# Filter taps of the long convolution: eight fp32 products become twenty-four single-pass products over 64 rows

## The reference, cut to what matters

```
hdn = sin(fr * (z @ w1 + b1)); hdn = sin(fr * (hdn @ w2 + b2)); hdn = sin(fr * (hdn @ w3 + b3))
h = (hdn @ wout).reshape(length, 2, D_HYENA)         # hdn 512x64, wout 64x1024: the taps
h = h * exp(-t * deltas)[:, None, :]
kern = concatenate([h[:, 0], zeros((1, D_HYENA)), h[:0:-1, 1]], axis=0)
```

## Time and profile before

| what | value |
|---|---|
| median of 3 runs | 1593.58 us (1593.38, 1593.58, 1594.43) |
| profiled execution, span from its first to its last instruction | 1591.6 us (what lies around it is not shown; the median of the runs is 2.0 us more) |
| PE busy | 1582.3 us, 99% |
| DVE, ACT, POOL busy | 62%, 48%, 38% |
| mean granted TensorE clock | 0.999 |
| the stage of the change (step (2, 0) to the sum at (3, 1)) | about 893 to 934 us of the span |

### The profile page before, as it was taken

How to read it: one execution, slowest core, us unless ns; L and a number is a source line. 1 busy time by engine, 2 the same in 40 slices (tenths; PEclk the granted TensorE clock), 3 DMA queues, 4 the chain that set the end, 5 groups by cost and what they waited for, 6 DMA issues and landing times.

```text
span 1591.6 us, 21844 instructions
## 1 busy us (share of the span) xinstructions
PE 1582.3 (99%) x8856; PEld 1360.9 (86%) x8856; DVE 994.1 (62%) x1477; ACT 761.6 (48%) x1143; POOL 603.8 (38%) x301
## 2 busy tenths in 40 slices
PE   9999999999999999999999999999999999999998
PEld 7888898889888888888888777889888789999997
DVE  7888867676765365455553767782356785555554
ACT  7533443343432334555556465424435645555554
POOL 1003112221245334455556333453223225555552
PEclk9999999999999999999999999999999999999999
DMA  6554434343466423233333332132112233232321
GB/s 245 172 172 147 142 117 140 113 132 126 128 214 213 149 70 117 95 106 106 104 96 137 126 120 66 53 107 83 40 54 67 80 106 107 93 106 93 106 93 54
DMA packets 54413, 182.95 MB, mean 115 GB/s; under 512 B 6556, under 2 KB 7196, under 8 KB 53928
## 3 DMA queue, kind: packets, MB, share of 16 engines
q1 hardware_dynamic: 54024, 181.02, 34.6%
q10 hardware_dynamic: 288, 0.52, 0.1%
HBM read 174.42 MB, written 3.96 MB: 112 GB/s over the span
## 4 chain that ended last, share of the span: by engine, by line
PE 92%; DVE 5%; ACT 1%; issue 1%; DMA 0%; SPq 0%; POOL 0%; DVEq 0%; ACTq 0%
PE banks L468 90%; PE banks L471 2%; DVE ACC L1300 1%; DVE wl L1264 1%; DMA maskf<-cst_dram 0%; DVE TM L1858 0%; DVE X L1233 0%; DVE HL L1233 0%; ACT T L2205 0%; DVE XW L2105 0%; ACT wh L2208 0%; ACT HH L2205 0%; DVE banks L1233 0%; DVE TM L1868 0%; ACT FHI L2208 0%
## 5 line engine op out<-in xcount | busy, mean ns | idle before, releaser
L2858 POOL TENSOR_TENSOR wl<-raw,wh 128x1024 fp32r<-128x1024 f32 x139 | 346.8, 2498 | 388.1 <-ACT wh L2208 388.0
L468 PE MATMUL banks<-HH,wh 128*128 128x512 f32 (+2 forms) x944 | 362.2, 386 | 1.3 <-ACT HH L2205 1.0
L468 PE MATMUL banks<-HL,wh 128*128 128x512 f32 (+2 forms) x944 | 353.1, 380 | 0.1
L2208 ACT ACTIVATE wh<-raw 128x1024 fp32r<-128x1024 f32 x246 | 257.3, 1051 | 188.6 <-PE banks L468 184.6
L468 PE MATMUL banks<-HH,wl 128*128 128x512 f32 (+1 forms) x936 | 251.4, 380 | 0.5 <-DVE wl L1264 0.5
L468 PEld LDWEIGHTS banks<-HH,wh 128*128 128x128 f32 (+1 forms) x944 | 177.2, 188 | 38.5 <-issue 2.6
L468 PEld LDWEIGHTS banks<-HL,wh 128*128 128x128 f32 (+1 forms) x944 | 176.6, 188 | 35.5 <-DVE HL L1233 1.7
L468 PEld LDWEIGHTS banks<-HH,wl 128*128 128x128 f32 x936 | 172.1, 188 | 35.8 <-issue 1.5
L468 PE MATMUL banks<-wh,HH 128*128 128x256 f32 x448 | 127.8, 285 | 0.0
L468 PE MATMUL banks<-wl,HH 128*128 128x256 f32 x448 | 126.7, 283 | 0.0
L468 PE MATMUL banks<-wh,HL 128*128 128x256 f32 x448 | 126.7, 283 | 0.0
(11 more groups left out here) (432 smaller groups left out, 3300.1 us busy)
## 6 DMA issues: line engine op xcount, KB each, us to landing
raw<-wst_dram SPq DMA_DIRECT2D x294, 512.0 KB, 3.4
X<-xT_dram SPq DMA_DIRECT2D x8, 512.0 KB, 6.1
CB<-sums_dram SPq DMA_DIRECT2D x12, 256.0 KB, 3.1
D<-dec_dram SPq DMA_DIRECT2D x12, 256.0 KB, 2.9
x_dram<-X SPq DMA_DIRECT2D x3, 512.0 KB, 6.4
QS<-QX SPq DMA_DIRECT2D x24, 64.0 KB, 2.6
KSw<-KX SPq DMA_DIRECT2D x24, 64.0 KB, 2.0
X<-x_dram SPq DMA_DIRECT2D x3, 512.0 KB, 4.6
```

The lines of the kernel that those rows point to most:

```text
L468: return pe.eng.matmul(dst, w, x, start=start, stop=stop, skip_group_check=True)
L2208: return eng.activation(dst, src, ACT.Copy)
L2858: tt(wl[:, q, :], raw[:, i % NRAW, :], wh[:, q, :].bitcast(F32), ALU.subtract).then_inc(*by_pool("low", u))
```

## The change

FO is loaded folded: rows 0 to 63 hold the weights of the forward direction and rows 64 to 127 those of the backward one, 128x512 in place of 128x1024. The third layer's weights and the small vectors are doubled, so that the 64 features stand in FH twice, in rows 0 to 63 and again in rows 64 to 127. After the third sine ACT makes high halves of FH and FO (FHH, FOH). At step (2, 0), ahead of the first taps, DVE makes the low halves (FOL, FHL), in place of FO and FH. PE then makes each block of taps with six fp32r products over 64 rows: for each of high x high, low x high and high x low, one for each direction, side by side.

```
--- before.py
+++ after.py
@@ -358,7 +358,9 @@
 
     UR, US = at("UR", [128, 4, T], C0), at("US", [128, 4, T], C0 + 8)
     FW = at("FW", [128, 3, 128], C0 + 18)
-    FO, FH, EN = at("FO", [128, 1024], 156), at("FH", [128, T], 160), at("EN", [128, T], 162)
+    FO, FH, EN = at("FO", [128, T], 156), at("FH", [128, T], 160), at("EN", [128, T], 162)
+    FOH, FOL = at("FOH", [128, T], 158, F32R), at("FOL", [128, T], 156, F32R)
+    FHH, FHL = at("FHH", [128, T], C0 + 28, F32R), at("FHL", [128, T], 160, F32R)
     FA, FZ, DEL = at("FA", [128, T], C0 + 26), at("FZ", [128, T], C0 + 34), at("DEL", [128, T], C0 + 36)
     A1 = at("A1", [128, T], C0 + 16)
     FTH, FTL = at("FTH", [128, 4, 2, 256], 124, F32R), at("FTL", [128, 4, 2, 256], 132, F32R)
@@ -848,10 +850,15 @@
             free[2] = (done("layer kept", l),)
 
         def filter_taps(t):
+
+            for n, (h, o) in enumerate(((FHH, FOH), (FHL, FOH), (FHH, FOL))):
+                for d in range(2):
+                    rows = slice(64 * d, 64 * d + 64)
+                    pe.wait_ge(done(("sine high", "sine low", "fo low")[n]), done("fo high"), *free[2 + d])
+                    i = mm(bank[2 + d], h[rows, 128 * t:128 * t + 128], o[rows, :], n == 0, n == 2)
+                    if n == 2:
+                        i.then_inc(*by_pe("taps", t, d))
             for d in range(2):
-                pe.wait_ge(done("sine", 2), done("fo"), *free[2 + d])
-                mm(bank[2 + d], FH[:, 128 * t:128 * t + 128], FO[:, T * d:T * d + T], True,
-                   True).then_inc(*by_pe("taps", t, d))
                 free[2 + d] = (done("decayed", t, d),)
 
         def filter_norm():
@@ -1691,6 +1698,12 @@
             dve.wait_ge(by_dve.last())
             ts(FH[:, :], FH[:, :], PI_BELOW, -PI_BELOW, ALU.min, ALU.max).then_inc(*by_dve("phase", l))
 
+        def lows_of_taps():
+            dve.wait_ge(done("fo high"))
+            tt(FOL[:, :], FO[:, :], FOH[:, :].bitcast(F32), ALU.subtract).then_inc(*by_dve("fo low"))
+            dve.wait_ge(done("sine high"))
+            tt(FHL[:, :], FH[:, :], FHH[:, :].bitcast(F32), ALU.subtract).then_inc(*by_dve("sine low"))
+
         def filter_taps(t):
             dve.wait_ge(done("taps", t, 0), done("window", t), by_dve.last())
             tt(FA[:, :], bank[2], FZ[:, :], ALU.mult).then_inc(*by_dve("decayed", t, 0))
@@ -1728,6 +1741,7 @@
             steps[at_step] = [lambda i=i: filter_layer(i)]
         for i, at_step in enumerate(((2, 0), (2, 1), (2, 2), (3, 0))):
             steps[at_step] = [lambda i=i: filter_taps(i)]
+        steps[(2, 0)].insert(0, lows_of_taps)
         steps[(2, 1)].insert(0, lambda: taps_low(0))
         steps[(2, 2)].insert(0, lambda: taps_low(1))
         steps[(3, 0)].insert(0, lambda: taps_low(2))
@@ -2507,6 +2521,11 @@
         def filter_layer(l):
             act.wait_ge(done("phase", l))
             fn(FH[:, :], FH[:, :], ACT.Sin).then_inc(*by_act("sine", l))
+            if l == 2:
+                act.wait_ge(by_act.last(), done("r squared", 11))
+                copy(FHH[:, :], FH[:, :]).then_inc(*by_act("sine high"))
+                act.wait_ge(done("fo"))
+                copy(FOH[:, :], FO[:, :]).then_inc(*by_act("fo high"))
 
         def filter_taps(t):
             act.wait_ge(done("del"), done("decayed", t - 1, 1) if t else done("layer", 2))
@@ -3241,11 +3260,12 @@
     for k, v in (("g0", n["norm_g"][0]), ("g1", n["norm_g"][1]), ("gm", n["mem_norm_g"]), ("gf", n["final_norm_g"]),
                  ("gmix", n["norm_mix_2"][0]), ("gmlp", n["norm_mlp_2"][0]), ("gfin", n["norm_final_2"]),
                  ("bada", n["b_ada_2"][0]), ("cb", n["conv_b_2"][0]), ("hb", n["hyena_bias_2"][0]),
-                 ("gn", n["gla_norm_2"][0]), ("bf", n["fox_b_f"][0]), ("c", n["c_2"]), ("cc", n["c_ctx_2"]),
-                 ("fr", n["filt_freq_2"])):
+                 ("gn", n["gla_norm_2"][0]), ("bf", n["fox_b_f"][0]), ("c", n["c_2"]), ("cc", n["c_ctx_2"])):
         put(k, feats(v, PAR[k][1]))
     put("cw", n["conv_w_2"][0].reshape(3, 12, 128).transpose(2, 0, 1).reshape(128, 36))
     put("fb", np.stack([feats(n["filt_b%d_2" % i], 1)[:, 0] for i in (1, 2, 3)], 1))
+    put("fr", np.tile(n["filt_freq_2"].reshape(64, 1), (2, 1)))
+    par[64:, PAR["fb"][0] + 2] = n["filt_b3_2"].reshape(64)
     par[:, PAR["nt"][0]:PAR["nt"][0] + 4] = -np.linspace(0.0, 1.0, T, dtype=f32).reshape(256, 2).T.reshape(4, 128).T
 
     fox = n["fox_w_in"][0]
@@ -3274,9 +3294,8 @@
     fw = np.zeros((128, 3, 128), f32)
     fw[:33, 0, :64] = n["filt_w1_2"][0]
     fw[:64, 1, :64] = n["filt_w2_2"][0]
-    fw[:64, 2, :64] = n["filt_w3_2"][0]
-    fo = np.zeros((128, 1024), f32)
-    fo[:64] = n["filt_wout_2"][0]
+    fw[:64, 2, :64] = fw[:64, 2, 64:] = n["filt_w3_2"][0]
+    fo = np.concatenate([n["filt_wout_2"][0][:, :T], n["filt_wout_2"][0][:, T:]], 0)
     gkw = np.zeros((128, 2, 256), f32)
     for o in (0, 32):
         gkw[o:o + 16, 0] = n["gk_w_fwd_2"][0]
```

## The result

In nine executions each, the changed kernel's median is **1597.55 us** (1596.76 to 1598.37) and that of the kernel before 1593.45 (1593.03 to 1594.84): a ratio of 1.0024, 95% interval 1.0016 to 1.0033. The change makes the kernel 4.1 us slower. The profiled execution spans 1595.3 us, 3.7 more than before. The prediction's 1596.3 was 1.3 short; its range, 1594.0 to 1598.8, holds the result.

The account below looks back on a forecast made before the run. PE was taken to bound the kernel, with DVE nearly as late: +4.1 in the first block less 3 x 0.63 gave +2.2, DVE's EN made it +2.7, so 1593.6 + 2.7 = 1596.3 us; range 1594.0 to 1598.8.

Parts of the forecast that it names:

- a block of taps: At PE's taps: three pairs at 0.23 plus 0.39 make 1.08 us for 1.71, saving 2.5 in four blocks.
- FOL begins, FHL ends: On DVE ahead of the window products: FOL starts at 900.3; FHL, held by POOL, ends at 903.75.
- PE stands: In the first block of taps, PE waits for FHL from about 899.2 to 903.8, about 4.6 us.
- PE alone at the end of the fourth block: After the taps: +4.1 in the first block less 3 x 0.63 saved, +2.2 us, without DVE's chain.
- (A): Main case: the long wait at the taps with no clock loss, 1596.3 us, own range 1595.7 to 1597.0; chance 0.42.
- (B): Behind the wait at the taps: standing PE loses its clock, 2.2 us more, +4.9, 1598.5; chance 0.25.
- Rival C: On DVE: FHL slips in before POOL or is not held, PE resumes at 901.7; +0.7, 1594.3; chance 0.20.
- D: At the taps: low halves ready when PE comes, gain is the 0.5 of slack, 1593.1; chance 0.05.
- E: At the taps: pairs run one after another, 1.77 a block, 1598.3 with the long wait; chance 0.03.
- the 0.39 of the rows: Around the 64-row pairs: going in and out costs 0.09 + 0.11 + 0.08 + 0.11 us, read from ret_scores.
- the 0.5 at EN: At EN's last sum: DVE's chain, started 3.1 later, ends at 935.7 after PE's own 935.2, making +2.7.
- without any new wait, DVE's chain would let PE gain 0.5 of its 2.5: At EN, DVE's slack of 0.5 us was taken as the most the change can bring.

Follow-up runs that it names:

- e11: Kernel before plus the milder relief of DVE alone (taps_low of blocks 1 and 2 to step (3, 0), EN's sum later); 1594.10 us, ratio 1.0004.
- e9: e5 plus the milder relief of DVE (taps_low of blocks 1 and 2 to step (3, 0), EN's sum later); 1591.50 us, ratio 0.9987.
- e3: Changed kernel, with PE filling the wait for FHL in the first block with 18 products into a bank nobody reads; 1595.82 us, ratio 1.0013.
- e5: Changed kernel with its new operations hidden: FOH, FOL at step (1, 0), FHH at (1, 3), FHL between squares of X blocks; 1593.54 us, ratio 0.9999.
- e2: Folded layout with two fp32 products over 64 rows side by side, without the changed kernel's halves, copies and subtractions; 1593.41 us, ratio 0.9999.
- e1: Changed kernel with both low halves moved on DVE ahead of the sums of squares, behind the additions to X at n = 1; 1596.03 us, ratio 1.0015.
- e4: Changed kernel with FHL made before FOL, splitting the wait in two; 1597.71 us, ratio 1.0024.
- e6: e2 plus the first relief of DVE: all four taps_low at step (3, 1), filter_norm at (3, 2); 1595.36 us, ratio 1.0010.
- e8: e5 plus the first relief of DVE: all four taps_low at step (3, 1), filter_norm at (3, 2); 1593.93 us, ratio 1.0003.
- e7: Kernel before plus the first relief of DVE alone: all four taps_low at step (3, 1), filter_norm at (3, 2); 1596.31 us, ratio 1.0016.
- e10: e2 plus the milder relief of DVE (taps_low of blocks 1 and 2 to step (3, 0), EN's sum later); 1592.28 us, ratio 0.9992.
- e12: e9 with each block's six products ordered one direction after the other; 1591.74 us, ratio 0.9988.

## Why the prediction was right and where it was wrong

| step of the prediction | forecast | measured |
|---|---|---|
| a block of taps; the saving in four | 1.08; 2.5 | 1.07; 2.60 (e11 less e9) |
| weight copy on ACT later | 1.2 | 1.4, of which 0.2 was there before the copies |
| FOL begins, FHL ends | 900.3, 903.75 | 900.42, 903.85 |
| PE stands | about 4.6 from 899.2 | 4.41, released by DVE's FHL |
| PE alone at the end of the fourth block | +2.2 | +2.2 with the clock kept up (e3) |
| EN ends, and adds to PE's lateness | 935.7, +0.5 | 936.50 (934.94 in e3), +0 |
| clock | stays (A) | falls (B), 3.5 us long: +1.5 in the span |
| sum | +2.7 | +3.7 in the span, +4.1 timed |

**The wait was right in every part**: its place, cause and length. Rival C fell, since FHL missed its slot before POOL by 0.22 us, D since DVE was in its sums until 900.5, and E since the pairs are 0.23 apart. The Trainium skill's page, weighed against the earlier trace rows in the prediction, gives no cost around the pairs (the Trainium skill, "TensorE: Matmul & The Clock Gate", Part 3); the blocks of 1.07 and the 2.60 between e11 and e9 speak for the 0.39 of the rows.

**The step that failed is the choice of the likeliest case**: "PE stands from about 899.2 to 903.8" was forecast, and with it (A) at 0.42 over (B), "the standing PE loses its clock", at 0.25. The two share their condition, and B's text says so: "It decides if the wait is as long as (A) says". Given that wait, no row of before spoke for a clock that stays, and the nearest row spoke for the fall. So did the rule of the Trainium skill that stands with (B) in the prediction. I gave the case without the fall more weight, which nothing in the profile bore out. So the total was near and the range held, but in the case that was called likeliest the clock was wrong. B's price was 2.2 and the fall cost 1.5 in the profiled execution: from 903.91 to the next `OH,wl` product (908.06) is 4.15 us, in e3 the same way (903.92 to 906.53) takes 2.61, and all products were back at full speed after about 3.5 us instead of eleven products. The Trainium skill's rule, that an idle TensorE goes back to half its clock, holds in this case after a stand of 4.41 (the Trainium skill, "TensorE: Matmul & The Clock Gate", Part 1).

**The second term that failed is the 0.5 at EN.** I let DVE's steps from the first window product to EN keep their durations and lengthened their start by 3.1. Two things on that way did not keep. One is USL, at 912.41 in the earlier trace rows, which POOL had held for 2.86. With DVE later and POOL's order changed, its successor in the changed kernel begins at 917.35, 0.02 ahead of POOL, and takes 0.69; this time POOL is the one held, 2.93 instead of 2.54:

```profile
917.35 0.69 DVE L1726 TENSOR_TENSOR USL<-US,USH 128x512 fp32r<-128x512 f32 x1
...
917.37 2.93 POOL L2877 TENSOR_TENSOR wl<-raw,wh 128x1024 fp32r<-128x1024 f32 x1 [4.76 <-ACT wh L2222]
```

That frees 2.2 us of DVE, of which 1.3 goes into a wait for PE's third block. The other is the second addition into X at the end of n = 2. It waits for PE's bank, and did so in the kernel before:

```profile
920.55 0.69 DVE L1541 TENSOR_TENSOR X<-X,banks 128x512 f32<-128x512 f32 x1 [0.54 <-PE banks L468]
```

In the changed kernel:

```profile
925.03 0.69 DVE L1548 TENSOR_TENSOR X<-X,banks 128x512 f32<-128x512 f32 x1 [1.05 <-PE banks L470]
```

What lies behind this addition, EN too, follows PE's arrival there and not DVE's start. In e3, where the clock stays up, EN ends at 934.94, 2.4 later than before and not 3.1, and PE comes after it, at 935.27. How much of this is USL and how much the addition stays open; no run varied POOL's order by itself. By luck, then, the two errors have opposite signs: -0.5 and +1.5 in the span.

The remark that "without any new wait, DVE's chain would let PE gain 0.5 of its 2.5" was right in kind: e5 measured 0.15 below the kernel before, and the saving of 2.6 did not show. The place was wrong. It isn't EN at (3, 1) but X at the end of n = 2 where PE has 0.2 us of room, as e2, e5 and e1 show with waits of 1.1, 1.7 and 3.0 there.

**The clock over all executions** fits this. Each has a mean granted clock with three digits; the kernel before never fell under 0.999 in the 99 executions beside the experiments.

| kernel | longest new stand of PE, us | executions at 0.998 or less |
|---|---|---|
| changed | 4.4 | 6 of 9 |
| e4 | 1.7 and 2.3 | 9 of 11 |
| e1 | 3.0 | 9 of 11 |
| e6 | 2.2 | 6 of 11 |
| e8 | 2.2 | 3 of 11 |
| e7 | 1.8 | 1 of 11 |
| e5 | 1.7 | 0 of 11 |
| e2 | 1.1 | 0 of 11 |
| e3, e9, e10, e11, e12 | none of size | 0 of 55 |

The digits are coarse: the profiled execution of the changed kernel, with its 3.5 us at half clock, shows 0.999, so the counts are rather too low. The means say more. They are 0.9981 for the changed kernel and 0.9994 for the kernel before beside e1 to e4; the difference of 0.0013 in 1593 us is 2.1 us of full clock, an estimate. That is near the 1.9 by which the changed kernel and e3 differ when each is set against its own runs of before (4.1 less 2.2). So 4.1 is **2.2 of stand less saving, and 1.5 to 1.9 of clock**.

Open: why a stand of 2.2 dropped the clock in the profiled execution of e6 and not in that of e8, and what sets the length of the fall. No run varied this by itself.

## What to carry to other kernels

Work that prepares the operands of a cheaper product must be placed where its engine has room before the product is due: here the same arithmetic is 4.1 us slower or, hidden and with DVE's order eased, 2.1 us faster. Before costing such a change, ask which engine empties PE's banks next; PE's saving counts only up to that engine's slack, 0.2 us here. And price a stand of the matrix engine of a few us twice, once for its length and once for the clock behind it, which only a timeline or a narrow window shows.

## What the runs showed of the hardware

- **The same stand of PE costs its clock in some executions and not in others**: with single stands of 1.8, 2.2, 2.2 and 3.0 us the mean granted clock is 0.998 or less in 1, 3, 6 and 9 of 11 executions (table above). The profiled executions show it directly: the products behind a stand of 2.20 are 0.43 apart (e6), behind one of 2.22 they are 0.23 apart (e8). One pair of products between stands of 1.66 and 2.26 didn't save the clock (e4), 18 products in place of the stand did (e3).
- **Two fp32 products over 64 rows go side by side**: a block of two takes 1.24 instead of 1.71, with no split into halves (e2).
- **PE ran its two row halves out of the program's order, over three products**: in e12 the fourth product starts 0.01 us after the first, ahead of the second and third.
- **0.02 or 0.22 us decide over 2.2 us.** A DVE subtraction with both inputs in SBUF that begins 0.22 after POOL's takes 2.83 instead of 0.68, and one that begins 0.02 before it takes 0.69 while POOL's takes 2.93 (2.40 when nothing holds it). The Trainium skill, "SBUF — State Buffer", "SBUF: two separate sides", states it as a lock that goes to whichever starts first, for the whole instruction; the trace agrees. A small instruction is held as well: in e8 one on four columns takes 2.36 us beside POOL, 0.28 in the kernel before.
